# Two tiles of the first mixer side by side ahead of the first expert pass, with shared weight loads, in a two-block transformer kernel on one core

## The chip, the core and the metric

The kernel runs on one core of one Trainium2 chip. A core has five engines with instruction streams of their own: PE (TensorE, matrix products), DVE (VectorE), ACT (ScalarE), POOL (GpSimd, here the issuer of two kinds of DMA) and SP (SyncE, here the issuer of all other DMAs). Sixteen DMA engines move data from HBM, the chip's memory, to SBUF, the memory beside the engines. PE writes to PSUM, which has 8 banks. Engines wait for each other by semaphores only, and each runs its own instructions in order. The metric is the time of one execution on the device, in microseconds (us).

## What is computed

256 tokens of width 1024 pass through two layers of a first block and two layers of a second block. The change touches only layer 0 of the first block, whose layer is, cut to what matters:

```
cond = silu(c)
for l in range(2):
    mod = cond @ w_ada[l] + b_ada[l]              # 6144 wide: sh1, sc1, g1, sh2, sc2, g2
    h = rms_norm(x, norm1_g[l]) * (1 + sc1) + sh1
    proj = h @ w_in[l]                            # 1024 x 1280
    p, q, k, v = ...                              # pooled part, 8 query heads, 2 key heads, 2 value heads
    y = concat(pool(p), attention(norm(q), norm(k), v))   # causal, window of 128 tokens
    x = x + g1 * (norm(y) @ w_out[l])             # 1024 x 1024
    h2 = rms_norm(x, norm2_g[l]) * (1 + sc2) + sh2
    # expert part: 8 heads, each picks 16 of 16384 experts for each token
    s = (h2 @ wq[l]) . subkeys[l]                 # wq: 1024 x 2048, 256 columns for a head
    expert, gate = top 16 of the pair sums of top 16 of each half of s, softmax
    a = gelu(h2 . u[expert]) * gate
    x = x + g2 * sum over 128 picks of a * v[expert]
```

The row of `u` and the row of `v` of an expert lie together, 8 KB in all.

## The kernel before

**Tiles and passes.** The tokens are two tiles of 128, one on the 128 partitions each. Layer and tile make four passes p = 0 to 3, for (l, t) = (0,0), (0,1), (1,0), (1,1) (`TILES`). A pass has 128 steps. In step b one indirect DMA, issued by POOL, gathers for each of the 128 tokens the 8 KB of its b-th expert: 1 MB. DVE makes the dot product with `u` (one custom instruction over 1024 columns), ACT does gelu, the gate, and a diagonal matrix `DG`, and PE adds the gated `v` rows to two PSUM banks (`PS<-BIG,DG`, two matmuls of 512 columns). After the four passes comes the second block, which the change doesn't touch.

**What must be there before a pass.** For tile (l, t) a mixer (`pre`: norm, projection in five pieces of 256 columns, attention, pooling, output in four pieces, second norm) and then eight heads (`head`: 16 matmuls with `wq`, two with the subkeys, the top-16 search on DVE, the expert numbers `EID` and the gates). Steps 16h to 16h+15 of a pass gather the experts of head h. So two heads must be done when a pass begins, and the other six are made during it.

**The order of the work.** `drive` is run once by each engine's program. It advances Python generators (`pre`, `head`, `early`, `late`, `enter`) by one step at a time, and a table `WHEN` says at which step of a generator each piece of it is put out. So all engines get the same hand-made interleaving. Before the passes, `drive` runs the mixer of (0,0), which has 79 steps, and the first two heads, with the modulation work `early` between them. In pass p it runs the six remaining heads of its own tile (appended at b = 1, 17, ..., 81), the mixer of the next tile (appended at b = 2 or 4) and the next tile's first two heads (at b = 92 and 106).

**The modulation.** `mod` of both layers needs 48 blocks of `w_ada` of 1 MB each (`ADA`), numbered 0 to 47 here. POOL issues their loads ahead of all gathers. PE consumes them one by one: 24 for layer 0 (`matvec`, eight matmuls of 256 columns, followed by a `spread` from `ACC` that needs DVE or ACT in between), and 24 for layer 1 (`row`, eight matmuls that add to one bank).

**The rings.** `w_ada` blocks and gathers share a ring of 9 slots of 1 MB (`in_g`, `GSLOTS`: eight in the tensor `BIG`, one in `MOD`). Load n waits until PE has consumed entry n-9. The weights of mixers and heads (`win`, `wout`, `wq`, 1 MB each, and the small `mg` and `poolw`) and the two score tiles of a mixer share a ring of four slots (`in_w`, `WSLOTS`), filled by SP in order; each entry carries the name of the PE instruction that frees its slot. In the profile a line of a helper stands for many operations (PE L513 is every matmul, ACT L966 every copy, DVE L1303 every product or sum of two tensors), so rows are told apart by their tensors: `PS<-BIG,HT` with 256 columns is a projection or an output piece, `PS<-BIG,PARB` a `matvec` or `row`, `PS<-ACC,ONES` a `spread`, `PS<-HT,BIG` a head, L592 transposes of `H`, L625 transposes of the attention weights.

## Time and profile before

| | us |
|---|---|
| median of three runs | 2364.1 |
| lowest and highest | 2360.09 and 2368.74 |
| the profiled execution's own time | 2370.28 |
| its span from the first to the last instruction | 2368.5 |

The profile is one profiled execution. Its page gives busy time by engine, and the span in 40 slices with the share of time that the 16 DMA engines were busy and the GB/s that they moved. A timeline gives instructions in order of time: start, duration, engine, line, operation, output<-input, and in brackets the idle time of the engine before it and what ended it. A matmul in fp32 stands as two records, so that a group of eight matmuls reads "x16". The mean granted TensorE clock is 0.963 of full speed. The whole program moves 767.01 MB.

### The profile page before, as it was taken

What the parts mean: (1) busy time and instruction counts of PE and PEld (TensorE: products, weight loads), DVE (VectorE), ACT (ScalarE), POOL (GpSimd) and SP (SyncE); (2) the same over time, 40 slices, a digit from 0 to 9 for tenths busy, and PEclk for the clock granted to TensorE, in tenths of its full rate; (3) what the DMA queues carried; (4) which work ended last, traced back from release to release, by engine and by line L of the source; (5) the groups of instructions that cost most, each with busy time, mean ns of one, the idle gap of its engine ahead of it and who ended that gap; (6) DMA issues with size and microseconds to landing.
All of it is one profiled execution on the core that took longest, in us unless ns stands there. A gap on an engine that the chain in (4) does not pass through costs nothing.

```text
span 2368.5 us, 24191 instructions
## 1 busy us (share of the span) xinstructions
...
## 2 busy tenths in 40 slices
...
GB/s 381 417 395 427 426 427 427 427 427 420 426 427 411 426 427 417 426 422 426 424 427 405 427 427 427 416 369 110 154 157 149 171 131 76 108 194 109 171 102 18
DMA packets 107711, 767.01 MB, mean 324 GB/s; under 512 B 12210, under 2 KB 12482, under 8 KB 15939
## 3 DMA queue, kind: packets, MB, share of 16 engines
...
## 4 chain that ended last, share of the span: by engine, by line
PE 58%; DMA 25%; DVE 9%; ACT 5%; issue 2%; POOL 0%; DVEq 0%; ACTq 0%; POOLq 0%
PE PS L513 56%; DMA BIG<-in_uv,EID 22%; DVE BIG L1620 3%; DMA BIG<-in_wada 3%; ACT DG L966 1%; DMA MOD<-in_uv,EID 1%; ACT L1149 1%; DVE BIG L1313 1%; DVE SC L1389 1%; PE PS L625 1%; PE PS L592 1%; ACT AV L966 1%; ACT BIG L1035 0%; DVE X L1303 0%; DVE BIG L1299 0%
## 5 line engine op out<-in xcount | busy, mean ns | idle before, releaser
L513 PE MATMUL PS<-BIG,DG 128*128 128x512 f32 x1820 | 888.8, 625 | 159.7 <-ACT DG L966 141.2
L1620 DVE CUSTOM_DVE_ANT_0 BIG<-BIG,H 128x1024 f32<-128x1024 f32 x455 | 558.1, 1227 | 357.7 <-DMA BIG<-in_uv,EID 327.8
L454 POOL DMA_INDIRECT BIG<-in_uv,EID x455 | 510.1, 1121 | 766.7 <-PE PS L513 744.1
L513 PEld LDWEIGHTS PS<-BIG,DG 128*128 128x128 f32 x1820 | 332.3, 195 | 611.2 <-issue 297.2
L513 PEld LDWEIGHTS PS<-HT,BIG 128*128 128x128 f32 x2304 | 350.3, 193 | 76.4 <-issue 47.8
L513 PE MATMUL PS<-HT,BIG 128*128 128x128 f32 (+1 forms) x2304 | 383.6, 323 | 7.3 <-DVE HT L1299 3.5
L1149 ACT ACTIVATE AV<-AV 128x1 f32<-128x1 f32 x512 | 103.2, 201 | 666.9 <-DVE AV L1620 662.9
L513 PE MATMUL PS<-BIG,HT 128*128 128x256 f32 (+3 forms) x1216 | 299.7, 404 | 10.6 <-DVE HT L1299 3.6
L513 PE MATMUL PS<-BIG 128*128 128x512 f32 (+7 forms) x792 | 282.4, 528 | 1.8 <-DVE BIG L1299 1.8
L513 PEld LDWEIGHTS PS<-BIG,HT 128*128 128x128 f32 x1216 | 230.9, 196 | 80.0 <-issue 48.8
L1303 DVE TENSOR_TENSOR BIG<-BIG 128x256 f32<-128x256 f32 (+1 forms) x96 | 49.4, 515 | 383.5 <-ACT BIG L1284 381.3
L966 ACT ACTIVATE DG<-CST,AV 128x128 f32<-128x128 f32 x512 | 205.5, 401 | 48.9 <-ACT AV L966 1.5
L513 PEld LDWEIGHTS PS<-BIG 128*128 128x128 f32 (+3 forms) x792 | 134.6, 194 | 128.8 <-issue 124.0
L966 ACT ACTIVATE AV<-AV,GATE 128x1 f32<-128x1 f32 x512 | 150.7, 294 | 18.6
L1284 ACT ACTIVATE BIG<-PS 128x512 f32<-128x512 f32 x32 | 19.1, 597 | 383.9 <-PE PS L513 383.9
L513 PE MATMUL PS<-MOD,DG 128*128 128x512 f32 x228 | 113.8, 623 | 9.4 <-ACT DG L966 9.1
L1620 DVE CUSTOM_DVE_ANT_0 BIG<-MOD,H 128x1024 f32<-128x1024 f32 x57 | 70.1, 1229 | 41.0 <-DMA MOD<-in_uv,EID 36.8
L454 POOL DMA_INDIRECT MOD<-in_uv,EID x57 | 66.6, 1168 | 72.8 <-PE PS L513 69.0
L966 ACT ACTIVATE BIG<-PS 128x256 f32<-128x256 f32 (+6 forms) x122 | 52.9, 446 | 85.9 <-PE PS L625 45.9
L513 PEld LDWEIGHTS PS<-MOD,DG 128*128 128x128 f32 x228 | 42.8, 199 | 67.0 <-issue 39.5
L1149 ACT ACT_TABLE_LOAD x52 | 66.7, 1283 | 0.9
L513 PE MATMUL PS<-BIG,PARB 128*32 128x256 f32 x688 | 54.5, 453 | 13.4 <-DMA BIG<-in_wada 9.8
...
## 6 DMA issues: line engine op xcount, KB each, us to landing
BIG<-in_wada POOLq DMA_DIRECT2D x43, 1024.0 KB
BIG<-in_win SPq DMA_DIRECT2D x36, 1024.0 KB, 6.0
BIG<-in_wup SPq DMA_DIRECT2D x32, 1024.0 KB, 6.9
BIG<-in_wdn SPq DMA_DIRECT2D x32, 1024.0 KB, 4.8
BIG<-in_wq SPq DMA_DIRECT2D x28, 1024.0 KB
BIG<-in_wout SPq DMA_DIRECT2D x24, 1024.0 KB, 5.4
...
MOD<-in_wada POOLq DMA_DIRECT2D x5, 1024.0 KB
```

What stands on the lines that cost most here:

```text
L454: pool.e.indirect_dma_start(out=slot(u), out_offset=None, in_=I[f"uv{l}"], in_offset=bass.IndirectOffsetOnAxis(ap=EID[:, t * 128 + j:t * 1 ...
L513: return pe.e.matmul(dst, a, b, start=start, stop=stop)
L592: p = pe.e.transpose(PS[:, bk, c * 128:(c + 1) * 128], H[:, t, (c4 * 4 + c) * 128:(c4 * 4 + c + 1) * 128], ident)
L625: p = pe.e.transpose(PS[:, bk, x * 128:(x + 1) * 128], P[:, i, kc * 128:(kc + 1) * 128], ident)
L966: return a.e.activation(dst, src, ACT.Copy, scale=scale)
L1149: a.e.activation(AV[:, j:j + 1], AV[:, j:j + 1], ACT.Gelu).then_inc(*up("a.gelu", p, b - 1))
L1284: a.e.activation(AT[:, b % 2], PS[:, singles.where[("up", l, b)], :].rearrange("p (i s) -> p i s", i=2), ACT.Relu).then_inc(*up("a.relu", ...
L1303: return v.e.tensor_tensor(dst, a, b, op)
L1313: return v.e.scalar_tensor_tensor(out=dst, in0=a, scalar=s, in1=b, op0=op0, op1=op1)
L1389: v.e.reduce_max(mx, src, AX).then_inc(*up("v.c"))
L1620: v.e.tensor_tensor_reduce(out=JD, in0=slot(u)[:, 0:1024], in1=H[:, t, :], scale=1.0, scalar=0.0, op0=ALU.mult, op1=ALU.add, accum_out=AV[ ...
```

## The change

- Before the passes both mixers of layer 0 run, that of tile 1 eleven steps behind that of tile 0 (`apart`). Its last two output pieces, its second norm and what follows come another 12 steps later (`behind`).
- The five pieces of `win` and the four of `wout` of layer 0 are loaded once, and a slot is freed by tile 1's use.
- The modulation's blocks are spread differently over the steps: nine in step 4, thirteen up to step 56, none in steps 57 to 71, then one in each step. The heads of tile 0 start at step 79 and step 89 of one common count of 102 steps.
- Pass 0 makes twelve heads in place of six, the mixer and two: those of tile 0 at b = 1, 17, ..., 81, and tile 1's heads 0 to 5 at b = 9, 25, ..., 89, each with the `wq` block of the tile-0 head just before it, which is not loaded again (`HEADS`, `BLOCK`, `LOADS`, `LAST_USE`). Pass 1 makes tile 1's heads 6 and 7 at b = 65 and 81, and the mixer and two heads of (1,0) as before.
- Before the passes `singles` may use PSUM bank 7 as well, until the first head needs it. Head buffers go by the order of the heads (`n % 2`), and the copy of a head's scores on ACT comes one step earlier.

```diff
+HEADS = [(0, 0, 0), (0, 0, 1)] + [x for h in range(6) for x in ((0, 0, h + 2), (0, 1, h))] + [(0, 1, 6), (0, 1, 7)] + [
+    (1, t, h) for t in range(2) for h in range(8)]
+BLOCK = {(l, t, h): h if t == 0 else (h + 2) % 8 if l == 0 else 7 - h for l, t, h in HEADS}
+LOADS = {(l, t, h): (l, 0, BLOCK[(l, t, h)]) if t == 1 and h < (6 if l == 0 else 2) else (l, t, h) for l, t, h in HEADS}
+LAST_USE = {LOADS[x]: x for x in HEADS}
...
+def behind(l, t, j):
+
+    return 12 if (l, t) == (0, 1) and j > 1 else 0
...
-                    load(in_w, ("win", l, t, j), I["win1"][l * 5 + j], 2048, ("pe.proj", l, t, j))
+                    if (l, t) != (0, 1):
+                        load(in_w, ("win", l, t, j), I["win1"][l * 5 + j], 2048, ("pe.proj", l, t if l > 0 else 1, j))
...
-                    yield from k.to(WHEN["out"] + 2 * j)
-                    load(in_w, ("wout", l, t, j), I["wout1"][l * 4 + j], 2048, ("pe.out", l, t, j))
+                    yield from k.to(WHEN["out"] + 2 * j + behind(l, t, j))
+                    if (l, t) != (0, 1):
+                        load(in_w, ("wout", l, t, j), I["wout1"][l * 4 + j], 2048, ("pe.out", l, t if l > 0 else 1, j))
...
-                if t == 0 or h > 1:
-                    load(in_w, ("wq", l, t, h), I["wq"][l * 8 + (h if t == 0 else 7 - h)], 2048,
-                         ("pe.q", l, t, h) if t > 0 or h < 6 else ("pe.q", l, 1, 7 - h))
+                if LOADS[(l, t, h)] == (l, t, h):
+                    load(in_w, ("wq", l, t, h), I["wq"][l * 8 + BLOCK[(l, t, h)]], 2048, ("pe.q", *LAST_USE[(l, t, h)]))
...
         def drive(pre, head, early, late, experts, finish, enter):
-            mixer = pre(0, 0)
-            for k in range(WHEN["T0"] + 1):
-                next(mixer)
-            for _ in range(9):
-                next(early, None)
-            for k in range(WHEN["T0"] + 1, WHEN["end"] + 1):
-                next(mixer, None)
-                if k in range(18, 57, 3) or WHEN["n2"] <= k < WHEN["n2"] + 3:
+            mixers, h0, h1 = (pre(0, 0), pre(0, 1)), head(0, 0, 0), head(0, 0, 1)
+            for k in range(WHEN["end"] + WHEN["head"] + 2):
+                for _ in range(9 if k == WHEN["T0"] + 1 else 1 if k in (18, 21, 26, 29, 32, 37, 40, 43, 46, 48, 50, 53, 56) or k > WHEN["n2"] else 0):
                     next(early, None)
-            h0, h1 = head(0, 0, 0), head(0, 0, 1)
-            for k in range(WHEN["head"] + 1):
-                next(h0, None)
-                if k >= 10:
+                next(mixers[0], None)
+                if k >= WHEN["apart"]:
+                    next(mixers[1], None)
+                if k > WHEN["end"]:
+                    next(h0, None)
+                if k > WHEN["end"] + 10:
                     next(h1, None)
-                if k >= 8:
-                    next(early, None)
...
                     if b % 16 == 1 and b < 96:
-                        live.append(head(l, t, 2 + b // 16))
+                        if p != 1 or b > 64:
+                            live.append(head(l, t, 2 + b // 16))
+                    elif p == 0:
+                        if b % 16 == 9 and b < 96:
+                            live.append(head(0, 1, b // 16))
...
-                yield from k.to(WHEN["sk"] + 3)
+                yield from k.to(WHEN["sk"] + 2)
```

**SP, from the first mixer weights on.** Before, in order (lines L325 are all `load`):

```order
L325 DMA BIG<-in_win 128x2048 x2
L325 DMA BIG<-in_mg 128x512
L325 DMA BIG<-in_poolw 128x512
L325 DMA BIG<-in_wout 128x2048 x4
L325 DMA BIG<-in_wq 128x2048 x3
L325 DMA BIG<-in_win 128x2048 x3
L325 DMA BIG<-in_wq 128x2048
L325 DMA BIG<-in_win 128x2048 x2
L325 DMA BIG<-in_mg 128x1024
L325 DMA BIG<-in_wq 128x2048
L325 DMA BIG<-in_poolw 128x512
L325 DMA BIG<-in_wq 128x2048
```

The same place in the changed kernel, where L336 is `load`:

```order
L336 DMA BIG<-in_win 128x2048 x2
L336 DMA BIG<-in_mg 128x512
L336 DMA BIG<-in_poolw 128x512
L336 DMA BIG<-in_mg 128x1024
L336 DMA BIG<-in_poolw 128x512
L336 DMA BIG<-in_wout 128x2048 x4
L336 DMA BIG<-in_wq 128x2048 x8
L345 DMA PARB<-in_par 128x2696
L336 DMA BIG<-in_win 128x2048 x5
```

The second set of `win` and `wout` is gone, and after `wout` only `wq` blocks come, until the weights of layer 1.

**PE, at the end of the first mixer's attention.** Before, the last `matvec` blocks (numbers 18 and 19), the transposes of `H`, the four output pieces, and the next two `matvec` blocks (20 and 21) stand like this:

```order
L513 MATMUL PS<-BIG,PARB 32x256 x8
L513 MATMUL PS<-ACC,ONES 128x256
L513 MATMUL PS<-BIG,PARB 32x256 x8
L513 MATMUL PS<-ACC,ONES 128x256
L592 MATMUL PS<-CST,H 128x128 x8
L513 MATMUL PS<-ACC,ONES 128x256
L513 MATMUL PS<-BIG,HT 128x256 x32
L513 MATMUL PS<-BIG,PARB 32x256 x16
```

In the changed kernel (L526 is every matmul, L640 the transposes of attention weights, L607 those of `H`), from block 18 to blocks 20 and 21:

```order
L526 MATMUL PS<-BIG,PARB 32x256 x8
L526 MATMUL PS<-ACC,ONES 128x256
L640 MATMUL PS<-CST,BIG 128x128 x8
L526 MATMUL PS<-PRJ,BIG 128x64 x8
L526 MATMUL PS<-BIG,PARB 32x256 x8
L526 MATMUL PS<-ACC,ONES 128x256
L607 MATMUL PS<-CST,H 128x128 x8
L526 MATMUL PS<-ACC,ONES 128x256
L526 MATMUL PS<-PRJ,BIG 128x64 x8
L526 MATMUL PS<-BIG,HT 128x256 x32
L607 MATMUL PS<-CST,H 128x128 x8
L526 MATMUL PS<-BIG,HT 128x256 x16
L526 MATMUL PS<-BIG,PARB 32x256 x16
```

Tile 1's attention, its transposes and two of its output pieces now stand ahead of block 20 too.

**DVE, in pass 0, where two heads overlap.** In the changed kernel, between two dot products (`ISA`, two rows each), stand the last parts of one head and the first of the next:

```order
L1638 ISA AV 128x1
L1321 TENSOR_TENSOR BIG<-BIG,CST 128x256
L1321 TENSOR_TENSOR BIG<-BIG 128x256
L1576 MAX TV<-BIG 128x8
L1578 MAX_INDEX TI<-TV,BIG 128x8
L1579 MATCH_REPLACE BIG<-TV,BIG 128x128
L1638 ISA BIG,AV<-BIG,H 128x1024
L1638 ISA AV 128x1
L1622 TENSOR_REDUCE BIG<-BIG 128x32
L1331 SCALAR_TENSOR_TENSOR EID<-BIG 128x16
L1582 MAX TV<-BIG 128x8
L1584 MAX_INDEX TI<-TV,BIG 128x8
```

Before, the same parts of a head stand with parts of the mixer around them, and no two heads share a step:

```order
L1620 ISA AV 128x1
L1303 TENSOR_TENSOR BIG<-BIG,CST 128x256
L1303 TENSOR_TENSOR BIG<-BIG 128x256
L1303 TENSOR_TENSOR BIG<-PRJ 128x640
L1488 TENSOR_REDUCE SC<-BIG 128x10
L1620 ISA BIG,AV<-BIG,H 128x1024
L1620 ISA AV 128x1
L1604 TENSOR_REDUCE BIG<-BIG 128x32
L1313 SCALAR_TENSOR_TENSOR EID<-BIG 128x16
L1620 ISA BIG,AV<-BIG,H 128x1024
```

## Rows read from the trace of the kernel before

**Rows 1.** The page: GB/s of the DMA engines in 40 slices.

```profile
GB/s 381 417 395 427 426 427 427 427 427 420 426 427 411 426 427 417 426 422 426 424 427 405 427 427 427 416 369 110 154 157 149 171 131 76 108 194 109 171 102 18
```

**Rows 2.** Stretches: us, busy us (count) by engine, PE clock, DMA share, GB/s.

```profile
0.00:50.00 50.00, 30.90 (x226) 22.46 (x227) 11.05 (x29) 9.55 (x20) 9.29 (x21) 0.93 0.96 372
50.00:110.00 60.00, 48.80 (x352) 31.92 (x351) 18.66 (x50) 15.20 (x45) 6.33 (x12) 0.89 1.01 427
110.00:140.00 30.00, 26.56 (x263) 19.12 (x265) 16.16 (x49) 6.26 (x14) 4.22 (x8) 1.00 0.91 348
140.00:180.00 40.00, 28.09 (x305) 10.35 (x296) 3.51 (x17) 1.67 (x2) 13.40 (x20) 0.70 1.01 425
180.00:1580.00 1400.00, 1231.28 (x3945) 638.20 (x3946) 1002.98 (x2414) 659.55 (x1900) 569.09 (x504) 0.97 1.01 424
```

**Rows 3.** The chain of waits at the passes' end: start, us, what.

```profile
1571.35 2.00 PE PS L513 x4
1573.78 2.00 PE PS L513 x4
```

**Rows 4.** The page's DMA issues: count, KB each, median us to landing.

```profile
BIG<-in_win SPq DMA_DIRECT2D x36, 1024.0 KB, 6.0
...
BIG<-in_wq SPq DMA_DIRECT2D x28, 1024.0 KB
BIG<-in_wout SPq DMA_DIRECT2D x24, 1024.0 KB, 5.4
```

**Rows 5.** POOL's timeline before the first pass: loads 28 and 29, first gather.

```profile
91.91 0.53 POOL L447 DMA_DIRECT2D BIG<-in_wada  x1 [1.64 <-PE PS L513]
116.99 0.53 POOL L447 DMA_DIRECT2D BIG<-in_wada  x1 [24.55 <-PE PS L513]
...
160.51 0.98 POOL L454 DMA_INDIRECT BIG<-in_uv,EID  x1 [2.11 <-PE PS L513]
```

**Rows 6.** PE's timeline, 35 to 178 us.

```profile
35.23 16.23 PE L513 MATMUL PS<-BIG,HT 128*128 128x256 f32 x64 [2.05 <-ACT HT L1071]
...
52.40 3.72 PE L513 MATMUL PS<-BIG,HT 128*128 128x256 f32 x16
...
66.35 2.14 PE L513 MATMUL PS<-BIG 128*128 128x128 f32 x16
...
73.55 0.96 PE L625 MATMUL PS<-CST,BIG 128*128 128x128 f32 x4 [2.35 <-ACT BIG L1035]
...
81.46 1.08 PE L513 MATMUL PS<-PRJ,BIG 128*128 128x64 f32 x8
...
88.34 1.07 PE L513 MATMUL PS<-BIG,PARB 128*32 128x256 f32 x16 [0.47 <-ACT MOD L966]
89.34 0.70 PE L513 MATMUL PS<-ACC,ONES 128*128 128x256 f32 x2
...
115.59 1.93 PE L513 MATMUL PS<-BIG,PARB 128*32 128x256 f32 x32
...
121.74 1.09 PE L592 MATMUL PS<-CST,H 128*128 128x128 f32 x8 [0.34 <-DVE H L1303]
...
177.75 1.94 PE L513 MATMUL PS<-BIG,PARB 128*32 128x256 f32 x16 [0.51 <-DMA BIG<-in_wada]
```

**Rows 7.** DVE's timeline: one softmax step, and two output pieces.

```profile
69.44 0.69 DVE L1389 TENSOR_REDUCE SC<-BIG 128x4 f32<-128x512 f32 x1
...
108.79 0.42 DVE L1303 TENSOR_TENSOR BIG<-PS,MOD 128x256 f32<-128x256 f32 x1 [2.51 <-PE PS L513]
...
112.24 0.42 DVE L1303 TENSOR_TENSOR BIG<-PS,MOD 128x256 f32<-128x256 f32 x1 [2.57 <-PE PS L513]
```

**Rows 8.** SP's timeline: the last two pieces of `win` before the mixer.

```profile
26.97 14.49 SPq L325 DMA_DIRECT2D BIG<-in_win  x2
```

**Rows 9.** DVE's timeline in pass 3, two steps with parts of one head.

```profile
1353.80 1.23 DVE L1620 CUSTOM_DVE_ANT_0 BIG<-BIG,H 128x1024 f32<-128x1024 f32 x1
...
1356.37 1.22 DVE L1620 CUSTOM_DVE_ANT_0 BIG<-BIG,H 128x1024 f32<-128x1024 f32 x1
```

More of the change, by code:

```diff
@@ L38 @@
 PROJ = (2, 3, 4, 0, 1)
+HEADS = [(0, 0, 0), (0, 0, 1)] + [x for h in range(6) for x in ((0, 0, h + 2), (0, 1, h))] + [(0, 1, 6), (0, 1, 7)] + [
[3 more added lines that the diff above has]
+LAST_USE = {LOADS[x]: x for x in HEADS}
 LAST = [GSLOTS[(len(ADA) + 512 + i) % len(GSLOTS)] for i in range(len(GSLOTS))]
 WHEN = dict(T0=3, proj=7, qk=17, qkT=22, pool=26, s0=30, pw=32, s1=34, pT0=36, pT1=40, pv0=41, pv1=45, T1=53, out=57,
-            n2=71, T2=74, end=78, sk=6, top=10, head=22, enter=88, rows=6)
+            n2=71, T2=74, end=78, sk=6, top=10, head=22, enter=88, rows=6, apart=11)
+def behind(l, t, j):
+    return 12 if (l, t) == (0, 1) and j > 1 else 0
 class Clock:
@@ L553, in spread @@
                 p.then_inc(*up("pe.adb", l, b))
+            singles.places = [4, 5, 6, 7]
             def early():
@@ L663, in pre @@
                     have_hT(l, t, 0)
-                    w = have(in_w, ("win", l, t, j))
+                    w = have(in_w, ("win", l, t if l > 0 else 0, j))
                     bk, freed = singles.take(("proj", l, t, j), (engine_of(i) + ".proj", l, t, j))
@@ L715, in pre @@
                 for j in range(4):
-                    yield from k.to(WHEN["out"] + 2 * j)
+                    yield from k.to(WHEN["out"] + 2 * j + behind(l, t, j))
                     have_hT(l, t, 1)
-                    w = have(in_w, ("wout", l, t, j))
+                    w = have(in_w, ("wout", l, t if l > 0 else 0, j))
                     bk, freed = singles.take(("out", l, t, j), ("v.out", l, t, j))
@@ L722, in pre @@
                     by_tokens(bk, t, w, 256).then_inc(*up("pe.out", l, t, j))
-                yield from k.to(WHEN["T2"])
+                yield from k.to(WHEN["T2"] + behind(l, t, 3))
                 transposes(l, t, 2, ("v.h2", l, t))
@@ L729, in head @@
                 sk = SKB.rearrange("p (a n) -> p a n", a=2)
-                wv = have(in_w, ("wq", l, t, h) if t == 0 or h > 1 else ("wq", l, 0, 7 - h)).rearrange("p (k n) -> p k n", k=8)
-                n = (l * 2 + t) * 8 + h
+                wv = have(in_w, ("wq", *LOADS[(l, t, h)])).rearrange("p (k n) -> p k n", k=8)
+                n = HEADS.index((l, t, h))
                 if n > 0:
-                    pe.wait_ge(*at("a.s", *TILES[(n - 1) // 8], (n - 1) % 8))
+                    pe.wait_ge(*at("a.s", *HEADS[n - 1]))
+                else:
+                    singles.places = [4, 5, 6]
+                    pe.wait_ge(*at(*singles.held[7]))
                 for i in range(2):
@@ L1116, in pre @@
                 evac_hT(l, t, 1)
-                yield from k.to(WHEN["n2"])
+                yield from k.to(WHEN["n2"] + behind(l, t, 3))
                 a.wait_ge(*at("v.out", l, t, 3))
                 rms_in_hT(f"n2{t}", ("n2", l, t), t, [X[:, t, :]], 1024.0)
-                yield from k.to(WHEN["T2"] + 2)
+                yield from k.to(WHEN["T2"] + 2 + behind(l, t, 3))
                 evac_hT(l, t, 2)
@@ L1532, in pre @@
                 for j in range(4):
-                    yield from k.to(WHEN["out"] + 2 * j + 3)
+                    yield from k.to(WHEN["out"] + 2 * j + 3 + behind(l, t, j))
                     v.wait_ge(*at("pe.out", l, t, j))
@@ L1540, in pre @@
                     stt(sc2, sc2, 1.0, par1("n2"), ALU.add, ALU.mult).then_inc(*up("v.c"))
-                yield from k.to(WHEN["n2"] + 2)
+                yield from k.to(WHEN["n2"] + 2 + behind(l, t, 3))
                 s = inverse(f"n2{t}", 1, ("n2", l, t))
@@ L1545, in pre @@
                 tt(H[:, t, :], H[:, t, :], sh2, ALU.add).then_inc(*up("v.h2", l, t))
-                yield from k.to(WHEN["T2"] + 3)
+                yield from k.to(WHEN["T2"] + 3 + behind(l, t, 3))
                 evac_hT(l, t, 2)
```

20 lines of the change are left out of this document (10 added, 10 removed).

## The prediction

> **What bounds the kernel now.** I read the page's GB/s line first [rows 1]. The reader is to see 427 GB/s or nearly so in the first 26 of 40 slices and less than half of it behind: until the last gather, near 1590 us, the 16 DMA engines set the pace, whatever PE and DVE do. The stretches say the same with numbers: 424 GB/s from 180 to 1580 us, PE busy for 1231 and DVE for 1003 of those 1400 us [rows 2]. The chain of waits shows it at the scale of a step: near the end of the passes a step is 1573.78 - 1571.35 = 2.43 us, of which PE has 2.00 [rows 3]; 1.0486 MB, a gather or one weight block, take 2.46 us at 427 GB/s. So a block that isn't loaded is worth 2.46 us, as long as the DMA engines have other work in its place. That is the whole question, and it is decided before the first pass. There I read POOL. It runs up to nine blocks of `w_ada` ahead of PE, and load 29 waited 24.55 us for PE to use block 20 [rows 5]. PE did that at 115.59 [rows 6]. The DMA engines hardly felt it, since a few loads were still queued: 427 GB/s until 110 us, 348 from 110 to 140, 425 after [rows 2]. Before 180 us they moved 50 x 0.372 + 60 x 0.427 + 30 x 0.348 + 40 x 0.425 = 71.6 MB. At the full rate from 50 us on it would be 18.6 + 130 x 0.427 = 74.1 MB, so only 2.5 MB or 5.8 us were lost. The first gather was issued at 160.51, while the last blocks still came in [rows 5]; the last one was used at 177.75 [rows 6].
>
> **What is removed.** Five `win` blocks, four `wout` and four `wq` of tile 1: 13 of the 36, 24 and 28 on the page [rows 4]. All of them were loaded between 0 and 1580 us, so 13 x 2.46 = 32.0 us go. PE, ACT and DVE do the same amount of work as before; what leaves pass 0 on them had been hidden under the transfers and gives nothing.
>
> **What is moved, and what it costs.** Tile 1's mixer now stands ahead of block 20 on PE, but for its last two output pieces. While PE hasn't used block 20, POOL can't issue load 29, and SP's ring of four slots is just as full: the `wq` blocks wait for tile 1's output pieces. At that point the DMA engines can have moved 29 + 5 + 4 = 38 blocks, or 39.8 MB, and some 4.4 MB of smaller things (x, constants, parameters, `mg`, `poolw`, by their shapes): 44.2 MB, which is 110 us at the rates above. Every us beyond that is idle. So I follow PE to block 20.
>
> The first three projections end as before. The first group of four took 16.23 us from 35.23 [rows 6], and at the steady pace of 112.24 - 108.79 = 3.45 us a piece [rows 7] the third ends at 48.1. From there to block 20, PE has: 7 more projections and 6 output pieces, 13 x 3.45 = 44.9; 12 `matvec` with their `spread`, 12 x (1.07 + 0.70) = 21.2 [rows 6]; three sets of eight transposes at 1.09, 3.3 [rows 6]; and the attention of two tiles. For tile 0 that is 2.14 for `poolw` and the first scores [rows 6], half of that for the second scores, two sets of transposes at 0.96 at most and two value products at 1.08 [rows 6], some 1.3 each for the query transposes and for pooling: 9.2. Tile 1 has twice the keys, so up to twice the matmuls in most of it; I take 13.8. The sum is 44.9 + 21.2 + 3.3 + 23.0 = 92.4 us, so that block 20 can't come before 48.1 + 92.4 = 140.5.
>
> To this come waits in the order that PE has now. (a) The fifth `win` block needs the slot of the first, which is now free only when tile 1 has used it, at 57, in place of 41 [rows 8] (the second of the two is issued 14.49 us behind the first). PE stands at its next projection until it lands. The bounds are 2.5 us (one block at the full rate) and 11 us (all that is queued on POOL's side first; before, the block was in use 11 us after its issue [rows 6, 8]); the median from issue to landing is 6.0 [rows 4], and I take 6.5 with its issue. (b) The softmax of tile 0: before, the transposes at 73.55 came 5.1 us after the scores' end at 68.5 [rows 6]; the second scores and the query transposes of tile 1 cover 1.9 of them: 3.2. (c) The softmax steps of tile 1, twice as wide: 0.69 us for the maximum becomes about 1.3 [rows 7], and DVE takes them in its own order, behind tile 0's row sums, `ACC` sums and products. PE waits 1.8 between the two scores, 0.7 and 4.5 ahead of the two sets of transposes. (d) ACT puts tile 0's squares and a table load ahead of the copies that tile 1's value products need: 2.1. (e) The copies into `HT` ahead of the output pieces and transposes: 1.9. Together 20.7, between 0 (each covered) and 40 (each twice as long). So block 20 comes at 161, 45 us later than before.
>
> Tile 1's first output piece ends one piece earlier, at 157.5, and frees a slot for `wq`; from there the queues are full again. 44.2 MB are moved by then, against 18.6 + 107.5 x 0.427 = 64.5: 20.3 MB, or 47.5 us of idle DMA. Behind it come 19 `w_ada` and 4 `wq` blocks, 23 x 2.46 = 57 us, so the first gathered rows land at about 215 in place of 180. I cost the rest at nothing: tile 1's last two pieces, its norm and the heads need less than 57 us and stand in that stretch; if they needed more, each us would count in full.
>
> In pass 0 twelve heads start 8 steps apart. DVE's step with a large part of one head takes 1356.37 - 1353.80 = 2.57 us [rows 9], hardly more than the 2.46 of a gather, and SP adds at least eight blocks in this pass (`wq` 4 to 7 and, with their slots free early, `win` of layer 1), which make the average step some 2.6 us on the DMA side. So DVE is near its limit without passing it: 0, with bounds 0 and 15. Passes 1 to 3 and the second block keep their work: 0, with 2 either way.
>
> **Sum.** -32.0 for the loads, +47.5 - 5.8 = +41.7 for the idle DMA, 0 for the passes: +9.7 us. On the profiled execution's own 2370.3 that is 2380. It lies 6.2 above the median of the runs, and the prediction goes by the median: 2364.1 + 9.7 = 2374. What a measurement can tell from no change is about 0.3%, 7 us, so this is just on the slow side.
>
> **Two rules weighed.** Rows first: the projection group that begins after an idle time took 16.23 us for four pieces, 2.4 more than at the pace of rows 7, and the granted clock is 0.70 in the stretch in which PE waits for blocks [rows 2, 6, 7]. The Trainium skill, TensorE: Matmul & The Clock Gate, section Why this matters for your kernels, says that idle gaps between bursts of matmuls bring the clock down to its lower level; the trace agrees. The case that it makes here is a rival below. On wait (a), where the rows leave 2.5 to 11 us, the skill's DMA: Bandwidth & Descriptors, section Queues, rings and completion order, says that each DMA engine takes turns between the queues that have work. By it SP's block would get half the rate beside POOL's, an estimate of 4.9 us and some latency, and the sum would stay within 1 us of mine.
>
> **The rivals.** (1) The two mixers cover each other's waits. For it: they are 11 steps apart, and PE's longest waits in the mixer of before were all for ACT or DVE, which the other tile's matmuls can fill. Against it: wait (a) is on a load, and DVE and ACT have one order for both tiles. With no wait left, block 20 comes at 140.5, the idle is 20.5 us less, and the time is 2353. It decides from about 144 on: block 20 earlier than that is faster by over 0.3%. (2) Half of the waits vanish, block 20 at 144 to 158: within 0.3%, about 2364. (3) The lower clock. Each of four longer waits (a, b, the 4.5 of c, d) is followed by 2.4 us more for PE, as in rows 6: +10, or 2384. Against it: with both tiles PE has fewer gaps than before. (4) DVE sets the pace in pass 0. If each of the 100 steps with heads took 2.75 us on DVE, 15 us come on top: 2389. Against it: the nine slots hold several gathers in flight, so DVE must fall far behind before the DMA engines notice. (5) That the loads don't go away is ruled out by SP's order above, where `wout` is followed by eight `wq` and no second `win`.
>
> **Chances.** Forecast 0.37, rival 1 0.21, rival 2 0.25, rival 3 0.12, rival 4 0.05. Faster is rival 1, 0.21; same is rival 2, 0.25; slower the rest, 0.54. The range runs from 2350 (no waits, and 3 us for the unknowns) to 2398 (waits of 20 us more, and some of DVE's), which leaves out less than 2 in 10.
>
> **What the profile will show.** Block 20's `matvec` and POOL's load 29 at about 161, after a wait of POOL of 25 to 30 us; a low in the GB/s line from about 70 to 157 us, with about 44 MB moved by 157; the first gathers' rows at about 215; on SP `win` x31, `wout` x20, `wq` x24; 424 GB/s from 220 us to the last gather, and that one about 10 us later than before. I am wrong if block 20 comes before 150 (rivals 1 and 2), if GB/s in pass 0 is under 420 (rival 4), or if the DMA engines find work between 110 and 157 that I have not seen.

## The result, and the profile after

| | before, us | after, us |
|---|---|---|
| median | 2364.5 (2360.09 to 2368.74, four runs) | 2382.9 (2382.04 to 2383.53, four runs) |
| the profiled execution's own time | 2370.28 | 2382.04 |
| its span | 2368.5 | 2380.2 |
| issue of the last gather | 1573.61 | 1593.22 |
| from there to the end of the span | 794.9 | 787.0 |

The median before now has a fourth run in it. The ratio of the times is 1.0078, with a 95% interval of 1.0059 to 1.0097: slower by 18.4 us. The forecast was slower by 9.7, at 2374, with a range of 2350 to 2398. The direction and the range held, and so did the mechanism: idle DMA engines before the first pass cost more than 13 loads save. The size was half of what came.

The page of the profile after, GB/s in 40 slices, and the issues of weight blocks (count, KB each, median us to landing); they answer [rows 1] and [rows 4]:

```profile
GB/s 366 265 188 426 427 427 427 427 425 426 426 427 411 423 427 409 426 425 427 422 426 400 427 427 427 427 404 163 115 185 151 142 165 60 121 192 109 168 106 18
...
BIG<-in_win SPq DMA_DIRECT2D x31, 1024.0 KB, 7.2
BIG<-in_wq SPq DMA_DIRECT2D x24, 1024.0 KB
BIG<-in_wout SPq DMA_DIRECT2D x20, 1024.0 KB, 5.4
```

The 13 blocks are gone (753.38 MB in all in place of 767.01), and the rate has fallen by a third in slice two (265 for 417) and by half in slice three (188 for 395), from 60 to 179 us. The stretches, in the columns of [rows 2]:

```profile
0.00:50.00 50.00, 29.19 (x218) 21.10 (x219) 10.43 (x29) 10.50 (x22) 9.72 (x21) 0.90 0.93 355
50.00:70.00 20.00, 10.64 (x60) 8.33 (x59) 5.79 (x12) 2.19 (x6) 0.53 (x1) 0.80 1.01 427
70.00:90.00 20.00, 20.00 (x127) 15.74 (x130) 3.60 (x6) 2.56 (x7) 1.05 (x2) 0.95 0.57 197
...
140.00:160.00 20.00, 17.66 (x94) 15.67 (x94) 7.92 (x15) 4.57 (x12) 0.00 (x0) 0.99 0.29 109
160.00:180.00 20.00, 19.04 (x161) 12.45 (x161) 6.67 (x12) 2.02 (x5) 3.12 (x6) 0.91 0.66 250
180.00:220.00 40.00, 32.28 (x352) 21.30 (x352) 13.19 (x44) 4.28 (x9) 9.81 (x17) 0.90 1.01 426
220.00:600.00 380.00, 330.52 (x1130) 162.05 (x1123) 303.31 (x815) 180.21 (x517) 164.70 (x144) 0.98 1.01 426
600.00:1590.00 990.00, 863.97 (x2640) 435.09 (x2638) 671.49 (x1553) 448.29 (x1319) 413.42 (x363) 0.96 1.01 422
```

From 180 us on the rate is that of before, pass 0 included. POOL's timeline shows where the idle time ends: its loads 28 and 29, which answer those at 91.91 and 116.99 in [rows 5], the first gather, and the last one. The last gather of before stands under them.

```profile
138.31 0.53 POOL L459 DMA_DIRECT2D BIG<-in_wada  x1 [12.93 <-PE PS L526]
170.20 0.53 POOL L459 DMA_DIRECT2D BIG<-in_wada  x1 [31.36 <-PE PS L526]
...
211.99 0.98 POOL L466 DMA_INDIRECT BIG<-in_uv,EID  x1 [6.01 <-DVE EID L1331]
...
1593.22 0.94 POOL L466 DMA_INDIRECT BIG<-in_uv,EID  x1 [1.54 <-PE PS L526]
```

```profile
1573.61 0.94 POOL L454 DMA_INDIRECT BIG<-in_uv,EID  x1 [1.51 <-PE PS L513]
```

DVE's first dot product in pass 0, which stood at 180.21 before:

```profile
233.97 1.23 DVE L1638 CUSTOM_DVE_ANT_0 BIG<-BIG,H 128x1024 f32<-128x1024 f32 x1 [5.19 <-DMA BIG<-in_uv,EID]
```

PE's way to block 20 (168.80; it answers 115.59 in [rows 6]), with its waits in brackets. The second line is the projection with the fifth `win` block:

```profile
37.43 12.54 PE L526 MATMUL PS<-BIG,HT 128*128 128x256 f32 x48 [2.05 <-ACT HT L1089]
...
68.32 5.55 PE L526 MATMUL PS<-BIG,HT 128*128 128x256 f32 x16 [9.36 <-DMA BIG<-in_win]
...
101.94 0.66 PE L640 MATMUL PS<-CST,BIG 128*128 128x128 f32 x4 [1.48 <-ACT BIG L1053]
102.53 1.74 PE L526 MATMUL PS<-BIG,PARB 128*32 128x256 f32 x16
...
116.49 1.99 PE L526 MATMUL PS<-BIG 64*128 64x256 f32 x8 [0.47 <-DVE BIG L1331]
...
128.77 1.09 PE L640 MATMUL PS<-CST,BIG 128*128 128x128 f32 x8 [3.62 <-ACT BIG L1053]
132.44 3.67 PE L526 MATMUL PS<-PRJ,BIG 128*128 128x64 f32 x16 [2.58 <-ACT BIG L984]
136.05 1.94 PE L526 MATMUL PS<-BIG,PARB 128*32 128x256 f32 x16
...
160.03 8.83 PE L526 MATMUL PS<-BIG,HT 128*128 128x256 f32 x32 [2.28 <-issue]
168.80 1.93 PE L526 MATMUL PS<-BIG,PARB 128*32 128x256 f32 x32
```

### The profile page after: what moved, and what is told of

The parts are those of the page before. It is cut to its first block, busy times and chain, and to the rows that moved or that the text cites. A ratio compares the mean times of both kernels' runs of the same rounds, so it can differ in the third digit from the quotient of the medians.

```text
span 2380.2 us, 24145 instructions
## 1 busy us (share of the span) xinstructions
PE 2116.7 (89%) x8236; PEld 1246.1 (52%) x8236; DVE 1228.9 (52%) x2911; ACT 807.9 (34%) x2336; POOL 609.0 (26%) x564
## 2 busy tenths in 40 slices
DMA packets 105839, 753.38 MB, mean 317 GB/s; under 512 B 12002, under 2 KB 12274, under 8 KB 15731
## 4 chain that ended last, share of the span: by engine, by line
PE 53%; DMA 26%; DVE 13%; ACT 5%; issue 2%; POOL 0%; DVEq 0%; ACTq 0%; POOLq 0%
PE PS L526 51%; DMA BIG<-in_uv,EID 22%; DVE BIG L1638 6%; DMA BIG<-in_wada 2%; DMA MOD<-in_uv,EID 2%; ACT DG L984 1%; DVE BIG L1321 1%; ACT L1167 1%; DVE BIG L1331 1%; DVE SC L1407 1%; PE PS L640 1%; PE PS L607 1%; DVE BIG L1317 1%; ACT AV L984 1%; ACT BIG L1053 0%
## 5 line engine op out<-in xcount | busy, mean ns | idle before, releaser
L526 PE MATMUL PS<-BIG,DG 128*128 128x512 f32 x1820 | 888.9, 624 | 159.3 <-ACT DG L984 146.9
L466 POOL DMA_INDIRECT BIG<-in_uv,EID x455 | 517.1, 1136 | 727.7 <-PE PS L526 694.0
L526 PEld LDWEIGHTS PS<-BIG,DG 128*128 128x128 f32 x1820 | 330.3, 195 | 627.2 <-ACT DG L984 325.8
L526 PEld LDWEIGHTS PS<-HT,BIG 128*128 128x128 f32 x2304 | 351.0, 193 | 75.1 <-issue 47.9
L526 PE MATMUL PS<-HT,BIG 128*128 128x128 f32 (+1 forms) x2304 | 384.6, 324 | 6.2 <-DVE HT L1317 3.5
L526 PE MATMUL PS<-BIG,HT 128*128 128x256 f32 (+3 forms) x1216 | 299.2, 404 | 21.3 <-DMA BIG<-in_win 9.4
L526 PE MATMUL PS<-BIG 128*128 128x512 f32 (+7 forms) x792 | 279.2, 523 | 2.2 <-DVE BIG L1317 1.7
L526 PEld LDWEIGHTS PS<-BIG,HT 128*128 128x128 f32 x1216 | 229.3, 195 | 87.3 <-issue 47.6
L526 PEld LDWEIGHTS PS<-BIG 128*128 128x128 f32 (+3 forms) x792 | 132.7, 192 | 127.3 <-issue 122.4
L526 PE MATMUL PS<-MOD,DG 128*128 128x512 f32 x228 | 113.0, 619 | 15.1 <-ACT DG L984 15.0
L526 PEld LDWEIGHTS PS<-MOD,DG 128*128 128x128 f32 x228 | 41.7, 195 | 73.8 <-issue 37.8
L526 PE MATMUL PS<-BIG,PARB 128*32 128x256 f32 x688 | 50.8, 426 | 15.4 <-DMA BIG<-in_wada 13.1
```

The source lines that it names most:

```text
L466: pool.e.indirect_dma_start(out=slot(u), out_offset=None, in_=I[f"uv{l}"], in_offset=bass.IndirectOffsetOnAxis(ap=EID[:, t * 128 + j:t * 1 ...
L526: return pe.e.matmul(dst, a, b, start=start, stop=stop)
```

## A measure that is cleaner than the time

Behind the last gather come the last steps of pass 3 and then the second block, with the same 3164 matmul records in each of the thirteen profiled executions. I call this whole stretch the second block. It took between 785.4 and 796.5 us. I compared the changed kernel with the kernel of the experiment `e4_fill3` below, which is the same there. Its matmuls run like those of the changed kernel until PE falls to its lower clock, at another place in each. PE's timeline of the changed kernel, 119 us and 505 us behind its last gather:

```profile
1712.18 3.67 PE L526 MATMUL PS<-MOD,BIG 128*128 128x64 f32 x16
1715.64 9.63 PE L526 MATMUL PS<-BIG,HT 128*128 128x256 f32 x32
...
2098.42 7.13 PE L526 MATMUL PS<-BIG,HT 128*128 128x256 f32 x32
```

and the same groups in the other kernel, whose last gather was issued at 1586.77:

```profile
1705.07 2.00 PE L526 MATMUL PS<-MOD,BIG 128*128 128x64 f32 x16
1706.90 7.12 PE L526 MATMUL PS<-BIG,HT 128*128 128x256 f32 x32
...
2096.01 9.32 PE L526 MATMUL PS<-BIG,HT 128*128 128x256 f32 x32
```

The first pair is slow in one and fast in the other, the last one the other way round. PE's granted clock in the 30 us around the first pair (the column ahead of the last two) was 0.82 in the changed kernel and 0.98 in the other:

```profile
1710.00:1740.00 30.00, 28.35 (x129) 21.53 (x127) 11.97 (x23) 11.50 (x34) 0.00 (x0) 0.82 0.35 140
```

```profile
1703.50:1733.50 30.00, 28.29 (x145) 20.61 (x146) 13.96 (x28) 14.55 (x41) 0.00 (x0) 0.98 0.44 175
```

Over the whole second block the mean granted clock was 0.99 in the three shortest executions (785.4, 787.0 and 787.2 us), 0.97 in the longest (796.5) and 0.98 in the nine between them. So the second block adds several us to a single execution for no reason that the change gives, and I read each experiment by the issue of its last gather as well as by its median. With it goes a sum, the prediction's own one: 2.46 us (1.0486 MB at 427 GB/s, taken unrounded) for each block loaded, plus the DMA engines' idle time from 50 to 240 us (190 us less 190 x GB/s / 427), plus what the first 50 us moved less than before (372 GB/s). Against the kernel before (5.8 idle, last gather at 1573.61):

| kernel | blocks | GB/s to 50 us | idle, us | sum, us | last gather | measured, us | median |
|---|---|---|---|---|---|---|---|
| changed | -13 | 355 | 56.1 | +20.4 | 1593.22 | +19.6 | 2382.9 |
| e1_fill | -13 | 357 | 57.8 | +21.9 | 1594.09 | +20.5 | 2391.9 |
| e2_own_wq | -7 | 361 | 56.1 | +34.4 | 1606.66 | +33.1 | 2398.6 |
| e3_own_mixer | -4 | 382 | 22.2 | +5.4 | 1578.93 | +5.3 | 2375.1 |
| e4_fill3 | -13 | 375 | 52.5 | +14.4 | 1586.77 | +13.2 | 2382.2 |
| e5_head_first | -4 | 339 | 20.5 | +8.8 | 1582.08 | +8.5 | 2372.4 |
| e6_head_first_nofill | -4 | 353 | 17.8 | +4.4 | 1576.75 | +3.1 | 2369.0 |
| e7_late_pieces | -13 | 350 | 56.1 | +21.0 | 1593.78 | +20.2 | 2388.2 |
| e8_fast_head_5 | -4 | 391 | 6.7 | -11.1 | 1561.83 | -11.8 | 2359.7 |
| e9_fast_head_2 | -4 | 375 | 10.7 | -5.3 | 1567.18 | -6.4 | 2363.2 |
| e10_waits_filled | -13 | 386 | 48.5 | +9.2 | 1580.80 | +7.2 | 2375.9 |
| e11_two_wout | -6 | 378 | 11.6 | -9.6 | 1561.54 | -12.1 | 2358.0 |

The sum meets eleven of twelve rows within 2 us, the last within 2.5. It is an account, not a forecast, since it takes each kernel's idle time from its own trace: what it shows is that nothing behind 240 us adds to the last gather, and so that the passes are no part of the loss. The median of before was 2362.8 to 2365.7 beside each of them. The rate of the first 50 us doesn't go by the edits: the kernels with shared `win` have the same instructions there and show 350 to 386, those with own blocks 339 to 391. In the changed kernel a `matvec` waited 2.95 us for its block there, in `e10_waits_filled` 1.10, and PE began the projection with the fifth `win` block at 68.32 in the one and at 64.66 in the other. The rates do go by the chip that a set of experiments ran on: 357 to 382 for `e1` to `e4` and `e11`, 339 to 353 for `e5` to `e7`, 375 to 391 for `e8` to `e10`. So the chip may set part of this, which no run here tests, and a comparison of last gathers between two sets is good only after the start is taken off.

## The experiments

All start from the changed kernel. `fills` below is the tuple of steps at which one `w_ada` block is used.

**Blocks used earlier.** Every step from 57 on, in place of from 72 on:

```diff
-... 50, 53, 56) or k > WHEN["n2"] else 0):
+... 50, 53, 56) or k > 56 else 0):
```

> The changed kernel, but the modulation's blocks 20 and up are used from step 57 on, one in each step, in place of from step 72 on: 15 blocks move ahead of the output pieces and transposes. Theory (the DMA engines stand idle before the first pass because POOL's ring waits for block 20): POOL's wait of 31 us goes, the low in GB/s from 70 to 170 us shrinks, the first dot product comes at 205 to 215 us in place of 234, and the time is 2355 (2350 to 2365), against 2383 for the changed kernel. Rival (pass 0 with twelve heads is what costs): nothing changes before the passes that matters, 2383. Rival (PE's own work sets the start): the mixers end later by what is put ahead, 2383 to 2390.

Measured: 2391.9 (ratio to before 1.0109, 1.0081 to 1.0137). The ring's long wait was gone, as meant, and nothing was won. POOL's last load and first gather, and DVE's rows between them:

```profile
187.56 0.53 POOL L459 DMA_DIRECT2D BIG<-in_wada  x1 [0.34 <-PE PS L526]
228.93 0.98 POOL L466 DMA_INDIRECT BIG<-in_uv,EID  x1 [40.84 <-DVE EID L1331]
```

```profile
210.41 0.42 DVE L1321 TENSOR_TENSOR BIG<-PS,MOD 128x256 f32<-128x256 f32 x1 [24.32 <-PE PS L526]
...
216.32 0.29 DVE L1576 MAX8 TV<-BIG 128x8 f32<-128x128 f32 x1
...
228.48 0.18 DVE L1331 SCALAR_TENSOR_TENSOR EID<-BIG 128x16 int32<-128x16 f32 x1
```

The 31 us of waiting at block 20 became 41 us of waiting for the first head's expert numbers. The time lies next to the third guess, that PE's own work sets the start (2383 to 2390). Here the theory that only the ring sets the idle time fell: there are two limits, the ring, and the chain over PE, the first head and DVE to `EID`. Some 9 us of the median stand against 0.9 us at the last gather; the rest is the second block, 796.5 against 787.0.

**Three blocks earlier.** `fills` with 57, 58 and 59.

> The changed kernel, but three blocks of the modulation (20, 21, 22) are used at steps 57 to 59, the rest as in it. Theory (ring of POOL): three more loads can be issued before the long wait, up to 3 x 2.46 = 7.4 us less idle time, so 2376 (2374 to 2380). Rival (pass 0, or PE's work): 2383, within 2 us.

Measured: 2382.2 (1.0080, 1.0053 to 1.0107), which looks like the rival. The last gather came 6.5 us earlier than in the changed kernel, and the second block took 793.2 in place of 787.0. Of the 6.5, 2.3 are the faster start (375 against 355 GB/s); the idle time behind it fell by 3.6, half of the theory's 7.4. So the theory holds for about half of its size, and one execution can't tell the rest from the rival. POOL waited 10.73 us for `EID` here, 6.01 in the changed kernel, and the DMA engines stayed busy over it; with fifteen blocks they ran dry (126 GB/s from 205 to 210 us, none from 225 to 230).

**Heads with their own blocks.** Six `wq` blocks are loaded again in the passes:

```diff
-... if t == 1 and h < (6 if l == 0 else 2) else ...
+... if t == 1 and h < (0 if l == 0 else 2) else ...
```

> The changed kernel, but tile 1's heads 0 to 5 load their wq blocks again: 6 blocks of 1 MB more, all within the passes. Theory (the DMA engines set the pace of the passes): 6 x 2.46 = 14.8 us more, 2398. Rival (DVE sets the pace of pass 0, where twelve heads stand): the loads hide, at most 5 us more, 2388.

Measured: 2398.6 (1.0144, 1.0115 to 1.0173), 15.6 us over the changed kernel, and 13.4 by the last gather. With the same twelve heads in pass 0, the same idle time (56.1) and nearly the same start, each block costs 2.2 to 2.6 us. The price of a block stands, and DVE hides behind the DMA engines in pass 0.

**The mixer with its own blocks.** Tile 1 loads `win` and `wout` itself:

```diff
-                    if (l, t) != (0, 1):
-                        load(in_w, ("win", l, t, j), ..., ("pe.proj", l, t if l > 0 else 1, j))
+                    load(in_w, ("win", l, t, j), ..., ("pe.proj", l, t, j))
```

> The changed kernel, but tile 1's mixer loads its five win and four wout blocks again: 9 blocks more, all ahead of the first pass. PE no longer waits for the fifth win block behind tile 1's first projection. Theory (the DMA engines are idle there anyway, PE's walk to block 20 sets the start): the 9 blocks cost next to nothing and the wait of 9.4 us and the lower clock behind it go, 2370 to 2383. Rival (every block counts 2.46 us wherever it stands): 22 more, 2405.

Measured: 2375.1 (1.0040, 1.0027 to 1.0054). Nine more loads, and 7.8 us faster than the changed kernel (14.3 by the last gather, of which 3.2 are the faster start). The stretches from 50 to 110 us:

```profile
50.00:70.00 20.00, 20.00 (x132) 15.70 (x130) 5.24 (x12) 1.91 (x5) 1.06 (x2) 1.00 1.02 427
70.00:110.00 40.00, 37.12 (x299) 26.51 (x292) 19.93 (x54) 13.21 (x45) 4.24 (x8) 1.00 1.01 420
```

PE doesn't wait in the first 20 of them (10.64 busy in the changed kernel), its clock stays at the upper level, and the nine loads pass while the DMA engines would have idled. The idle time falls by 33.9 us, from 56.1 to 22.2. The nine loads fill 22.1 of them, and the rest is block 20, which comes at 153.95, 14.8 us earlier. Sharing `win` in a ring of four slots brought a wait and saved nothing.

**Tile 1's pieces behind the first head.** With own loads, all four output pieces of tile 1 22 steps later, with five blocks more (`e5_head_first`) and without (`e6_head_first_nofill`):

```diff
-    return 12 if (l, t) == (0, 1) and j > 1 else 0
+    return 22 if (l, t) == (0, 1) else 0
...
-            live = [late, h1]
+            live = [late, h1, mixers[1]]
```

> As the run before, without the five earlier blocks. Theory: pieces 0 and 1 of tile 1 (8.8 us) no longer stand ahead of block 20 and of the first head, so block 20 at about 147 (155.4 with own loads alone) and the last gather at about 1570: 2364 to 2368. Rival (waits on ACT and DVE, not PE's place, set block 20): block 20 still at 153 or later, last gather at 1577 or later, 2373.

> Tile 1 has win and wout loads of its own, all its output pieces, its norm and what follows come 22 steps later (behind the first head's 16 matmuls, its last steps in pass 0), and five w_ada blocks are used at the steps 58, 61, 64, 67 and 70. Theory (before the first gather the time goes by the chain from PE's mixer work over T2 of tile 0 and the first head to EID, and by the ring of w_ada only while that chain leaves it idle): the DMA engines idle about 5 us before the first pass in place of 22 with own loads alone, the last gather is issued at about 1560 (1578.9 with own loads alone, 1573.6 before), time 2354 to 2359. Rival (blocks used earlier only push the chain to EID back, as all fifteen did): last gather at 1568 or later, time 2363 to 2370.

Measured: 2369.0 (1.0015, 0.9996 to 1.0033) and 2372.4 (1.0026, 1.0008 to 1.0045). Without the blocks, block 20 came at 148.1, as expected, but the last gather came 7 us later than expected; the slower start explains 3.4 of them (353 against 382 GB/s). The rest stays open: the idle time fell by only 4.4 us against `e3_own_mixer`. With five blocks the rival came true by the last gather (1582.08, expected at 1560). DVE's timeline in the kernel without them shows the flaw in both:

```profile
173.31 0.29 DVE L1580 MAX8 TV<-BIG 128x8 f32<-128x128 f32 x1
187.13 0.42 DVE L1319 TENSOR_TENSOR BIG<-PS,MOD 128x256 f32<-128x256 f32 x1 [13.13 <-PE PS L524]
...
202.84 0.17 DVE L1329 SCALAR_TENSOR_TENSOR EID<-BIG 128x16 int32<-128x16 f32 x1
```

The search of the first head was half done at 173.3, and then DVE stood at tile 1's first output piece, which is next in its order and which PE makes later. On PE I had put the head first, on DVE not. Without the five blocks this cost nothing, since `w_ada` loads kept the DMA engines at 426 GB/s from 170 to 220 us. With them POOL waited 30.17 us for `EID` in place of 14.34, and the rate fell to 346 from 190 to 220: what the blocks had won ahead was given back there.

**The same, with shared loads.** Only pieces 2 and 3, the norm and T2 (tile 1's transposes behind the norm) come ten steps later (`22 if (l, t) == (0, 1) and j > 1 else 0`, `live` as above).

> The changed kernel, shared loads, with only tile 1's output pieces 2 and 3, its norm and T2 ten steps later (behind the first head's search). The first head's MAX8 then doesn't wait for the pieces on DVE (199.4 before), nor EID for tile 1's norm. Theory: EID comes at about 200 and the first gather at 206, when POOL has issued its last w_ada load; but block 20 stays at 169 and the ring stays the limit, so the last gather is within 1590 to 1593 (1593.2), 2380 to 2383. Rival (the chain from the first head's projections to EID sets the time): first gather 10 us earlier, last gather at 1584 or earlier, 2373.

Measured: 2388.2 (1.0100, 1.0073 to 1.0128), last gather at 1593.78. The last gather stayed, within 1 us of the theory's range; the median missed its range by 5 us, of which the second block (790.2 against 787.0) explains 3. For the first gather both were wrong: 215.63. `MAX8` came 8 us earlier, at 191.22, and then DVE waited 13.56 us for an output piece of PE that stands just ahead of the last steps to `EID`. That `EID` came 3.6 us later and the last gather only 0.6 shows that in the changed kernel the chain to `EID` has that much slack, since the DMA engines still have `w_ada` blocks queued.

**Blocks inside waits of PE.** `fills` with 51 and 52, nothing else changed:

> The changed kernel with its shared loads and nothing but two w_ada blocks more at the steps 51 and 52, in PE's waits of 3.62 and 2.58 us. Theory (blocks used inside a wait of PE cost the chain nothing): two blocks, 4.9 us, less idle and the first gather where it was (212): last gather at 1588 (1593.2), 2376 to 2380. Rival (each block costs PE its 1.77 us also here): first gather at 215 and last gather at 1591 or later, 2381 or more.

Measured: 2375.9 (1.0057, 1.0042 to 1.0072), last gather at 1580.80, 12.4 us earlier than in the changed kernel, where the theory had 5. The faster start is 3.6 of them. The idle time fell by 7.6, more than the 4.9 of two blocks. The first gather came at 205.16, not at 212. PE's timeline, at the place where it waited 3.62 and 2.58 in the changed kernel:

```profile
125.38 1.13 PE L526 MATMUL PS<-BIG,PARB 128*32 128x256 f32 x16 [3.97 <-ACT MOD L984]
126.44 1.22 PE L526 MATMUL PS<-ACC,ONES 128*128 128x256 f32 x2
127.46 1.91 PE L640 MATMUL PS<-CST,BIG 128*128 128x128 f32 x8
...
129.85 1.90 PE L526 MATMUL PS<-PRJ,BIG 128*128 128x64 f32 x16
```

The first wait is still there (3.97), the second is gone, and the eight value products take 1.90 in place of 3.67, at the upper level of the clock. The two output pieces of tile 1 begin at 154.16, 5.9 us earlier, of which 3.7 were there at the projection with the fifth `win` block (64.66 against 68.32), and they take 7.14 us in place of 8.83. So two blocks cost PE nothing net here, and the other 2.2 us, with 1.7 at the pieces, are the lower clock and the wait that are gone.

**The first head fast.** Own loads and late pieces as above, and the first head by two steps in each common step, with `fills` 51 and 52 (`e9_fast_head_2`), and with 58, 61 and 64 too (`e8_fast_head_5`):

```diff
                 if k > WHEN["end"]:
                     next(h0, None)
+                    next(h0, None)
```

> Own loads and tile 1's output pieces behind the first head, as in the two runs before; the first head is advanced by two steps in each of the common steps, so that on DVE its EID stands ahead of tile 1's pieces (there it waited for them from 173 to 203 us); w_ada blocks are used at the steps 51 and 52, where PE waited 3.6 and 2.1 us for ACT, and at 58, 61 and 64. Theory: EID at about 185 to 190, no idle DMA behind 170 us, some 8 us idle in all from 110 to 170; last gather issued at 1563 to 1568 (before 1573.6, the changed kernel 1593.2), 2355 to 2360. Rival (the five blocks again cost what they bring, and the start's idle is set by PE's work alone): last gather at 1576 or later, 2369.

> As the run before with only the two blocks in PE's waits. Theory: 4.9 us less idle than without any (17.8) and nothing from the earlier EID, since the w_ada loads already kept the DMA engines busy from 150 us on: last gather at 1569 to 1573, 2361 to 2365. If EID alone had held it, the last gather would come at 1563.

Measured: 2359.7 (0.9981, 0.9969 to 0.9992) and 2363.2 (0.9997, 0.9984 to 1.0011), last gathers at 1561.83 and 1567.18. The stretches of the first, its `EID` and its first gather:

```profile
50.00:110.00 60.00, 56.31 (x419) 41.15 (x417) 25.49 (x64) 15.10 (x50) 5.82 (x11) 1.00 1.01 423
110.00:130.00 20.00, 16.93 (x137) 12.53 (x138) 7.12 (x19) 7.87 (x23) 1.94 (x4) 0.91 0.83 307
130.00:150.00 20.00, 18.28 (x156) 13.90 (x158) 10.98 (x19) 5.18 (x13) 2.29 (x5) 1.00 1.00 417
150.00:170.00 20.00, 15.65 (x221) 9.78 (x216) 8.18 (x36) 2.45 (x5) 6.34 (x12) 0.94 1.01 425
```

```profile
170.67 0.17 DVE L1330 SCALAR_TENSOR_TENSOR EID<-BIG 128x16 int32<-128x16 f32 x1
```

```profile
171.69 0.99 POOL L464 DMA_INDIRECT BIG<-in_uv,EID  x1 [4.33 <-DVE EID L1330]
```

With `EID` at 171 in place of 213 (in `e5_head_first`) the blocks used earlier are no longer given back, and 6.7 us of idle time are left of 56.1, though both mixers still stand ahead of the first pass. This version beats both kernels: 6 us less than before by the medians, 0.2% by the ratio, whose interval lies just clear of 1. The last gather is 11.8 us earlier than before. The sum says from where: 9.8 for the four `wq` blocks, 2.2 for the faster start, and 0.9 lost to idle. So by this sum the gain is that of the shared `wq`; the mixers side by side bring nothing of their own, they only no longer cost. `EID` came 15 us ahead of its range and the last gather 1 us. With two blocks the last gather came 2 us ahead of its range; the idle time fell by 7.1, not 4.9, much as in the run before this one, and the start was 2.6 faster than in `e6_head_first_nofill`.

**Two output blocks shared again.** Tile 1 uses its output columns in the order 2, 3, 0, 1, the first two with tile 0's blocks:

```diff
+def wout(l, t, j):
+    return ("wout", 0, 0, j + 2) if (l, t) == (0, 1) and j < 2 else ("wout", l, t, j)
```

> As the kernel with the fast first head and five blocks, but tile 1 begins its output with the two pieces of w_out that tile 0 used last and that still stand in the ring, so two wout blocks fewer are loaded, where there is hardly any idle DMA left. Theory (a block not loaded is worth 2.46 us where the DMA engines are busy, nothing where they idle): last gather 4.9 us earlier, at about 1557, 2353 to 2357. Rival (holding the two slots keeps wq back and opens the idle again): last gather at 1562 or later, 2360 or more.

Measured: 2358.0 (0.9972, 0.9952 to 0.9991), last gather at 1561.54, 0.3 us from the kernel with own blocks, or 1.8 if both starts are made equal. The theory's 4.9 us did not come. The stretch from 130 to 150 us answers the third one above:

```profile
130.00:150.00 20.00, 18.27 (x147) 13.69 (x146) 10.75 (x19) 4.60 (x12) 2.65 (x5) 1.00 0.77 310
```

It moved 20 x (0.417 - 0.310) = 2.1 MB less in it, just the two blocks, and the idle time rose from 6.7 to 11.6 us. So there was no hole at this place in the kernel with own blocks (417 GB/s); taking the loads away made one. SP's timeline shows why nothing moved up into it. First the kernel with own blocks, whose first two `wout` loads for tile 1 come at 138.5 and 142.0, then this one:

```profile
138.52 48.22 SPq L336 DMA_DIRECT2D BIG<-in_wout  x4
```

```profile
182.23 7.96 SPq L344 DMA_DIRECT2D BIG<-in_wout  x2
```

Two of the four slots hold the shared blocks, two hold `wq`, and SP can issue nothing from 136 to 182 us. That is the rival's mechanism (held slots open the idle again), at a last gather 0.5 us ahead of the rival's mark and a median 2 us below its 2360. A block that isn't loaded is worth its 2.46 us only if another load can take its place.

## Why the prediction was half right

**The bound: right.** The DMA engines set the pace up to the last gather, at 426 GB/s in pass 0 as well. Block loads in the passes are worth 2.46 us each (`e2_own_wq`).

**-32.0 for 13 blocks: right as a term of the sum** (see the table), though nine of them now fall into time that idles anyway; the -32.0 and the idle are two sides of one account. `e3_own_mixer` puts the nine back and loses nothing.

**PE's way to block 20, the mis-sized term: 161 forecast, 168.80 measured.** The waits were forecast at 20.7; measured, 9.36 (a) + 1.48 (b) + 0.47 + 0.47 + 3.62 (c, for 7.0) + 2.58 (d, for 2.1) + 2.28 (e, for 1.9) = 20.3. The sum is right because (a) was 2.9 too small and (b) and (c) 4.2 too large. For (a) the block was issued at 59.0 and used 9.3 us later, inside the bounds of 2.5 to 11, and well over the 4.9 and some latency of the estimate by turn-taking that the prediction weighed.

Two terms were missing. The third projection ended at 37.43 + 12.54 = 50.0, not 48.1: 1.9 of late start, which varies from execution to execution. And the lower clock behind the waits, at four places. The projection at 68.32 took 5.55 in place of the 3.62 at the upper level (+1.9). Behind the wait of 1.48, the `matvec` at 102.53 took 1.74 in place of 1.07, and its `spread` and the group `PS<-BIG,PRJ` behind it lost 1.0 more (+1.7). The value products at 132.44 took 3.67 in place of 1.90, the `matvec` at 136.05 took 1.94 in place of 1.07, and its `spread` and the transposes of `H` lost 1.4 more (+4.0). The two pieces at 160.03 took 8.83 in place of 7.07 (+1.8). That is 9.3 us; the upper-level times are those of the same groups elsewhere in this kernel and in `e8_fast_head_5`. Against it stands the work of PE. From 50.0 to 168.8 are 118.8 us; less the waits of 20.3 and these 9.3, 89.2 are left, where 92.4 were counted. (The terms listed there for tile 0's attention add up to 9.9, not to the 9.2 that went into the sum.) So 1.9 + 9.3 - 3.2 - 0.4 = 7.6 of the 7.8 that were off.

The lower clock was rival 3, priced at 10 us and given 0.12: its term came nearly in full. The Trainium skill's rule that I named for it (TensorE: Matmul & The Clock Gate, section Why this matters for your kernels) is that idle gaps between bursts of matmuls bring the clock down; the trace agrees, with the lower level behind waits of 9.36, 1.48, 2.58 and 2.28 us. It isn't so after each wait: `e8_fast_head_5` has the same wait of 1.48, and its `matvec` behind it took 1.07.

**The idle time: mis-sized with it.** 47.5 was forecast, and 55.9 us of idle between 50 and 220 us were measured (the stretches hold 48.7 MB, and 170 - 48.7 / 0.427 = 55.9), and 2.0 more from the slow start. The volume was right: 44.4 MB had been moved by 160 us, where I had counted 44.2. The point of resumption was wrong. I let the queues be full again from tile 1's first output piece, at 157.5. Yet from 160 to 180 us only 250 GB/s were moved, so that full rate came at about 168: one freed slot of SP is one block, and the ring of `w_ada` opens only with block 20. So the 7.8 us of block 20 and some 2.6 us of this too early resumption make the 55.9 + 2.0 - 47.5 = 10.4 that were missing. The first gathered rows, forecast at 215, were used at 233.97. Of these 19 us only the 10.4 cost anything: from 180 us on the DMA engines moved 426 GB/s, and what came ahead of the first rows didn't have to come behind them.

**The cost of the first head: nothing, as assumed,** but with less room than I took. The first gather was issued at 211.99, after 6 us for `EID`, while older loads kept the DMA engines at 426 GB/s. I had not looked at what DVE does ahead of `EID`. In the changed kernel this chain costs nothing; it is what keeps the idle time from being filled, as `e1_fill` and `e5_head_first` show.

**The second block: "0, with 2 either way" was wrong.** It lies between 785 and 797. The profiled execution of after was at 787.0, that of before at 794.9. So the own time, 2382.04 against the forecast of 2380, looks better than the sum was: +19.6 - 7.9 = +11.7. The medians show +18.4, nearer to what the last gathers say.

**The rivals.** 1 and 2 (waits covered) are out: the waits are there, 20.3 us. 3 came true in addition to the forecast, with 9.3 of its 10 us, and its 2384 is the time nearest to the measured 2382.9. That this one fits so well is in part luck: the resumption taken too early (2.6 us) and the work counted too high (3.2) cancel in it. 4 (DVE in pass 0) is out, 426 GB/s. 5 is out, by the counts on the page.

## What to carry to other kernels

Work that is put ahead of a streaming phase costs by the time at which the stream is full again, and the loads that it saves there are worth nothing if they would have fallen into that hole, or if a shared block holds the slot that the next load needs. Find every chain that holds the stream back (here two rings, PE's order and the first head on DVE), since opening one only hands the wait to the next; and when work is moved on one engine, look at what its results do to the order on the others. Where a later stage varies by itself, compare by a mark ahead of it.

## What the runs showed of the chip

The same instructions of the second block took 785.4 to 796.5 us, with a mean granted clock of 0.99 in the shortest and 0.97 in the longest execution. The fall to the lower level comes at different places in kernels that differ only some 1500 us earlier (the group 122 us behind the last gather took 9.63 in the changed kernel and 7.12 in `e4_fill3`). Before the first pass it followed waits as short as 1.48 us in one execution and not in another. The first 50 us moved 339 to 391 GB/s in four kernels with the same instructions there (`e3`, `e5`, `e6`, `e8`), which is 52 x 50 / 427 = 6 us; they ran on three chips, while kernels with own blocks on one chip lie up to 16 apart (`e8` 391, `e9` 375). Both are larger than many of the differences that one would like to read from a single median.
